# Products of the values for all chunks issued beside the first products of the levels, old state added by VectorE, last level on blocks of 32

## The reference

```python
def rwkv_scan(r, w, k, v, a, b, s0):
    def step(S, inp):
        r_t, w_t, k_t, v_t, a_t, b_t = inp
        sa = jnp.einsum('bhij,bhj->bhi', S, a_t)
        S = S * w_t[:, :, None, :] + sa[..., None] * b_t[:, :, None, :] + v_t[..., None] * k_t[:, :, None, :]
        return S, jnp.einsum('bhij,bhj->bhi', S, r_t)
...
def trunk_layer(x, l, v_first, past, p):
    h = x @ p['w_in'][l]
...
    merged = jax.nn.sigmoid(g_a) * (o_a @ p['w_up_a'][l]) + jax.nn.sigmoid(g_b) * (o_b @ p['w_up_b'][l])
    y = layer_norm(ALPHA * x + merged @ p['w_out'][l], p['ln_g'][l], p['ln_b'][l])
```

## Time and profile before

| | |
|---|---|
| Time, median of 3 runs | 2416.53 us (2414.43 to 2420.03) |
| Time of the profiled execution | 2419.8 us |
| Its span, first to last instruction | 2418.1 us |
| Busy: TensorE, VectorE, ScalarE | 2350.2, 610.7, 364.4 us |
| Mean granted clock of TensorE | 0.989 |

### The profile page before, as it was taken

How to read it: one execution, slowest core, us unless ns; L and a number is a source line. 1 busy time by engine, 2 the same in 40 slices (tenths; PEclk the granted TensorE clock), 3 DMA queues, 4 the chain that set the end, 5 groups by cost and what they waited for, 6 DMA issues and landing times.

```text
span 2418.1 us, 39663 instructions
## 1 busy us (share of the span) xinstructions
PE 2350.2 (97%) x17860; PEld 1906.4 (79%) x17860; DVE 610.7 (25%) x1076; ACT 364.4 (15%) x939; POOL 131.5 (5%) x233
## 2 busy tenths in 40 slices
PE   8999999999999999999899999999999999999995
PEld 7887878778787788888788778787787867888884
DVE  0132322217216410111201323222163153101112
ACT  0021111111113310000201211111201143100002
POOL 0000000002011110000000000000010112100000
PEclk9999999999999999999899999999999999999997
DMA  6532332327343354444244323323373334544441
GB/s 212 193 123 84 112 116 97 124 89 281 125 140 96 119 187 154 143 142 154 91 153 141 103 91 105 122 91 107 116 257 123 130 105 144 170 153 143 143 153 71
DMA packets 86793, 326.41 MB, mean 135 GB/s; under 512 B 11808, under 2 KB 11824, under 8 KB 84448
## 3 DMA queue, kind: packets, MB, share of 16 engines
q1 hardware_dynamic: 73152, 266.44, 33.8%
q0 software_dynamic: 13472, 57.43, 6.6%
HBM read 313.39 MB, written 18.82 MB: 137 GB/s over the span
## 4 chain that ended last, share of the span: by engine, by line
PE 94%; DVE 2%; ACT 2%; DMA 1%; issue 0%; POOL 0%; DVEq 0%; ACTq 0%; SPq 0%; POOLq 0%
PE PB L520 74%; PE PB L747 3%; PE PB L622 2%; PE PB L591 1%; PE PB L490 1%; PE PB L631 1%; DMA WT<-in_w_all 1%; PE PB L905 1%; PE PB L794 1%; PE PB L607 1%; PE PB L839 1%; PE PB L633 1%; ACT ARENA L914 1%; PE PB L652 1%; PE PB L659 1%; PE PB L644 0%
## 5 line engine op out<-in xcount | busy, mean ns | idle before, releaser
L520 PE MATMUL PB<-XT,WT 128*128 128x264 f32 (+1 forms) x6016 | 1426.9, 392 | 16.2 <-DMA WT<-in_w_all 7.8
L520 PEld LDWEIGHTS PB<-XT,WT 128*128 128x128 f32 (+1 forms) x6016 | 1118.4, 190 | 239.8 <-issue 37.5
L520 PE MATMUL PB<-H,WT 128*128 128x264 f32 x2048 | 456.5, 386 | 3.1 <-DVE H L1571 3.1
L520 PEld LDWEIGHTS PB<-H,WT 128*128 128x128 f32 x2048 | 389.0, 190 | 70.3 <-issue 3.8
L914 ACT ACTIVATE ARENA<-PB 128x512 f32<-128x512 f32 (+6 forms) x197 | 95.3, 500 | 410.0 <-PE PB L622 175.1
L1568 DVE SCALAR_TENSOR_TENSOR H<-H,PB 128x264 f32<-128x264 f32 x32 | 13.7, 429 | 305.2 <-PE PB L520 305.2
L392 POOL DMA_DIRECT2D out<-in_c_win x16 | 8.2, 510 | 1338.1 <-DVE ARENA L1327 1338.1
L1181 DVE COPY SHO<-PB 128x9 f32<-128x9 f32 x66 | 11.0, 167 | 266.5 <-ACT H L936 215.0
L1147 ACT ACTIVATE ARENA<-XT 128x1056 f32<-128x1056 f32 x8 | 8.7, 1083 | 458.5 <-DVE XT L1592 458.0
L936 ACT ACTIVATE H<-PB,PD 128x264 f32<-128x264 f32 x58 | 27.8, 479 | 275.2 <-PE PB L520 275.1
L951 ACT ACTIVATE H<-PB 128x264 f32<-128x264 f32 x64 | 24.9, 389 | 293.9 <-PE PB L520 293.7
(11 more groups left out here) (275 smaller groups left out, 1736.6 us busy)
## 6 DMA issues: line engine op xcount, KB each, us to landing
WT<-in_w_all SPq DMA_DIRECT2D x504, 512.0 KB, 4.7
out<-in_c_win POOLq DMA_DIRECT2D x16, 512.0 KB, 5.1
ARENA<-in_c_cmp POOLq DMA_DIRECT2D x64, 128.0 KB, 4.3
ARENA<-in_c_sel POOLq DMA_DIRECT2D x64, 128.0 KB, 3.4
ARENA<-in_c_win POOLq DMA_DIRECT2D x32, 256.0 KB, 3.6
ARENA<-in_states POOLq DMA_DIRECT2D x4, 1024.0 KB, 8.2
out<-ARENA POOLq DMA_DIRECT2D x4, 1024.0 KB, 5.4
ARENA<-in_w1d POOLq DMA_DIRECT2D x4, 1024.0 KB, 5.2
```

The source lines that it names most:

```text
L520: ins = mm(PB[0:m, bank, 0:T], WT[:, s, k, 0:m], x, start=start, stop=stop)
```

## The change

It does four things, all in the delta rule of the prompt.

The products of the values (lines 646, 661 and 671 before), which don't depend on the state, leave the chunks. A new function `of_values` issues them for all four chunks inside the `y` steps of levels 1, 2 and 3, one behind each product of the level, into banks 1, 2 and 3, where each chunk now has its own columns (`cq`). The chunks' own products add to what lies there (`start=False`).

The identity times the old state (line 663) is gone. VectorE multiplies the old state by the decay ahead of time (`d`, into `STD`), and after `s` computes decay times PSUM plus `STD` with two instructions of 128x64 (`stt`) in the place of one of 128x128.

The announcement of `s` comes behind 4 products in the place of 12. A chunk has 20 products in the place of 36.

The last level works on blocks of 32: its `y` and `z` steps have as many products as before, 16 each, but of 32x32. ScalarE copies half as much for it, and VectorE adds two pieces of 32 partitions.

```diff
-        assert used[0] <= at_chunks + 6400
+        LT = take(P, 2 * NCH, C)
+        RS, US, STD = take(P, 2, C), take(P, 2, C), take(P, 2, C)
...
               a="th exp sv tok0 tok1 x2 " + " ".join(f"y{j}" for j in lv) + " " + " ".join(f"r{c} u{c} o{c}" for c in ch),
               v=lambda it: ("lw one gate cum " + ("vd vg vm " if it >= NQUAD else "") + "kb kf kp rk at rt bt kt bon g40 g41 x0 x1 lm1 "
-                            + " ".join(f"lm{j + 1} z{j}" for j in range(1, LEVELS)) + f" z{LEVELS} st " + " ".join(f"s{c}" for c in ch)))
+                            + " ".join(f"lm{j + 1} z{j}" for j in range(1, LEVELS)) + f" z{LEVELS} st " + " ".join(f"d{c} s{c}" for c in ch)))
...
+                    def of_values(j, q, ra):
...
+                        w, c = divmod(q, NCH)
+                        k = (2 * w + 1) * NCH + c
+                        weights = {1: G4[ra, k, 0, :], 2: TOK[ra, 0, w, c, :], 3: TOK[ra, 2, w, c, :]}[j]
+                        x = G4[ra, k, 1, :] if j == 2 else TOK[ra, 0, w, c, :]
+                        return mm(PB[ra, j, q * C:q * C + C], weights, x, start=q == 0, stop=True, skip_group_check=True)
...
                     for j in lv:
                         wait(("rw_v", f"lm{j}" if j == 1 else f"z{j - 1}"))
...
+                        if j == 2:
+                            wait(("rw_a", "tok1"))
                         for q, ra in eight:
-                            ins = mm(PB[ra, 0, q * C:q * C + C], LM[other(ra), q, :], XX[other(ra), q, :], start=True, stop=True)
+                            oa = other(ra)
+                            if j < LEVELS:
+                                ins = mm(PB[ra, 0, q * C:q * C + C], LM[oa, q, :], XX[oa, q, :], start=True, stop=True)
+                            else:
+                                ins = mm(PB[low(ra), 0, q * C:q * C + 32], LM[up(oa), q, 32:C], XX[up(oa), q, 0:32], start=True, stop=True)
+                            if j <= 3:
+                                of_values(j, q, ra)
                         mark("rw_t", it, ins, f"y{j}")
                         project(L, hq, f"y{j}")
                         wait(("rw_a", f"y{j}"),)
...
                             for ra in both:
-                                ins = mm(PB[ra, 5, cols], YY[ra, q, :], XX[ra, 2 * NCH + q, :], start=True, stop=True)
+                                if j < LEVELS:
+                                    ins = mm(PB[ra, 5, cols], YY[ra, q, :], XX[ra, 2 * NCH + q, :], start=True, stop=True)
+                                else:
+                                    ins = mm(PB[up(ra), 5, q * C + 32:q * C + C], YY[low(ra), q, 0:32], XX[low(ra), 2 * NCH + q, 32:C],
+                                             start=True, stop=True)
                         mark("rw_t", it, ins, f"z{j}")
...
 
                     wait(("rw_a", "tok1"), ("rw_v", "st"))
                     for c in ch:
-                        pairs = [(w, slice(w * C, w * C + C)) for w in range(2)]
+                        pairs = [(w, slice((w * NCH + c) * C, (w * NCH + c + 1) * C)) for w in range(2)]
                         if c:
                             wait(("rw_v", f"s{c - 1}"))
-                        for w, cw in pairs:
+                        for w, cq in pairs:
                             for ra in both:
-                                mm(PB[ra, 0, cw], AR[ra, w * NCH + c, 0, :], ST[ra, c % 2, w, :], start=True, stop=False)
-                            for ra in both:
-                                ins = mm(PB[ra, 0, cw], G4[ra, (2 * w + 1) * NCH + c, 0, :], TOK[ra, 0, w, c, :], start=False, stop=True)
+                                ins = mm(PB[ra, 1, cq], AR[ra, w * NCH + c, 0, :], ST[ra, c % 2, w, :], start=False, stop=True, skip_group_check=True)
                         mark("rw_t", it, ins, f"r{c}")
                         project(L, hq, f"r{c}")
                         wait(("rw_a", f"r{c}"))
-                        for w, cw in pairs:
+                        for w in range(2):
                             for ra in both:
-                                ins = mm(PB[ra, 1, cw], XX[ra, (2 + w) * NCH + c, :], RS[ra, w, :], start=True, stop=True)
+                                ins = mm(PB[ra, 0, w * C:w * C + C], XX[ra, (2 + w) * NCH + c, :], RS[ra, w, :], start=True, stop=True)
                         mark("rw_t", it, ins, f"u{c}")
                         project(L, hq, f"u{c}")
                         wait(("rw_a", f"u{c}"))
-                        for w, cw in pairs:
+                        for w, cq in pairs:
                             for ra in both:
-                                mm(PB[ra, 3, cw], TOK[ra, 1, w, c, :], US[ra, w, :], start=True, stop=False)
+                                ins = mm(PB[ra, 3, cq], TOK[ra, 1, w, c, :], US[ra, w, :], start=False, stop=True, skip_group_check=True)
+                        mark("rw_t", it, ins, f"s{c}")
+                        for w, cq in pairs:
                             for ra in both:
-                                mm(PB[ra, 3, cw], TOK[ra, 2, w, c, :], TOK[ra, 0, w, c, :], start=False, stop=False)
+                                mm(PB[ra, 2, cq], ST[ra, c % 2, w, :], AR[ra, w * NCH + c, 1, :], start=False, stop=True, skip_group_check=True)
+                        for w, cq in pairs:
                             for ra in both:
-                                ins = mm(PB[ra, 3, cw], small(EYE)[ra], ST[ra, c % 2, w, :], start=False, stop=True)
-                        mark("rw_t", it, ins, f"s{c}")
-                        for w, cw in pairs:
-                            for ra in both:
-                                mm(PB[ra, 2, cw], ST[ra, c % 2, w, :], AR[ra, w * NCH + c, 1, :], start=True, stop=False)
-                            for ra in both:
-                                mm(PB[ra, 2, cw], US[ra, w, :], G4[ra, 2 * w * NCH + c, 1, :], start=False, stop=False)
-                            for ra in both:
-                                ins = mm(PB[ra, 2, cw], TOK[ra, 0, w, c, :], G4[ra, (2 * w + 1) * NCH + c, 1, :], start=False, stop=True)
+                                ins = mm(PB[ra, 2, cq], US[ra, w, :], G4[ra, 2 * w * NCH + c, 1, :], start=False, stop=True, skip_group_check=True)
                         mark("rw_t", it, ins, f"o{c}")
...
-                        mark("rw_a", it, copy(YY.rearrange("p q n -> p (q n)"), PB[:, 0, :]), f"y{j}")
+                        n = C if j < LEVELS else 32
+                        mark("rw_a", it, copy(YY[:, :, 0:n], PB[:, 0, :].rearrange("p (q n) -> p q n", n=C)[:, :, 0:n]), f"y{j}")
                         take_out(L, hq, f"y{j}")
                         take_out(L, hq, f"z{j}")
                     for c in ch:
                         wait(("rw_t", f"r{c}"))
-                        mark("rw_a", it, copy(RS.rearrange("p w n -> p (w n)"), PB[:, 0, 0:P]), f"r{c}")
+                        mark("rw_a", it, copy(RS[:, :, :], of_chunk(1, c)), f"r{c}")
...
-                        mark("rw_a", it, copy(US.rearrange("p w n -> p (w n)"), PB[:, 1, 0:P]), f"u{c}")
...
+                        mark("rw_a", it, copy(US.rearrange("p w n -> p (w n)"), PB[:, 0, 0:P]), f"u{c}")
...
-                        mark("rw_a", it, copy(H[:, hp:hp + 2, c * C:c * C + C], PB[:, 2, 0:P].rearrange("p (w n) -> p w n", n=C)), f"o{c}")
+                        mark("rw_a", it, copy(H[:, hp:hp + 2, c * C:c * C + C], of_chunk(2, c)), f"o{c}")
...
                         else:
-                            v(f"z{j}", tt(xt, xt, z[:, 2 * NCH:4 * NCH, :], ALU.add))
+                            for a in range(2):
+                                up = slice(a * C, a * C + 32)
+                                x = xt[up, :, 32:C]
+                                ins = tt(x, x, z[up, 2 * NCH:4 * NCH, 32:C], ALU.add)
+                            v(f"z{j}", ins)
...
-                        wait(("rw_t", f"s{c}"))
-                        v(f"s{c}", tt(ST[:, (c + 1) % 2], PB[:, 3, 0:P].rearrange("p (w n) -> p w n", n=C),
-                                      spread(decay[:, :, c], P, 2, C), ALU.mult))
+                        wait(f"s{c - 1}" if c else "st")
+                        v(f"d{c}", tt(STD[:, :, :], ST[:, c % 2], spread(decay[:, :, c], P, 2, C), ALU.mult))
+                        wait(("rw_t", f"s{c}"), f"d{c}")
+                        for w in range(2):
+                            ins = stt(ST[:, (c + 1) % 2, w, :], PB[:, 3, (w * NCH + c) * C:(w * NCH + c + 1) * C], GP[:, w * NCH + c, C:C + 1], STD[:, w, :],
+                                      ALU.mult, ALU.add)
+                        v(f"s{c}", ins)
                         mix(L, hq, f"s{c}")
```

More of the change, by code:

```diff
@@ L253, in hybrid_trunk @@
         KF = RK
-        used[0] = at_chunks + 6400
+        used[0] = at_chunks + 6528
         SV = take(P, 6, C)
@@ L260, in hybrid_trunk @@
         TOK = take(P, 6, NCH * C).rearrange("p (i w) (c n) -> p i w c n", w=2, n=C)
```

(7 more changed lines are left out.)

## The result

The changed kernel takes 2382.27 us (median of 4 runs, 2376.52 to 2383.60) and the kernel before 2417.97 us beside it. The ratio is 0.985 with a 95% interval of 0.9833 to 0.9867, so 36 us or 1.5% less. The forecast was 2380.4 us.

What follows compares the result with a forecast made beforehand. TensorE's own queue was taken as the bound, busy 2350.2 of 2418.1 us. Terms -30.0 + 0.2 - 6.9 + 0.6 = -36.1 us from the median 2416.53 gave 2380.4 us, range 2375.5 to 2391, at 80%.

Steps and rivals of the forecast that it cites:

- The chunks: Delta rule chunks: each of 32 loses 16 two-quarter products of 0.0585 us, 0.936 us a chunk, 30.0 us in all.
- The values: Steps y1 to y3: 16 added products alternate with the level's on four quarters, 1.09 for 1.08 us, 0.2 us in all.
- The rival in which they take turns with the level: Blocks y1 to y3: paired products go one at a time, 2.02 us a block, +22.5 us, so 2403; chance 5%.
- The last level: Steps y5 and z5: blocks of 32x32 products take 0.65 us in place of 1.08; 16 blocks save 6.9 us.
- The rule of the Trainium skill: Last level, kept as rival: some 60 cycles' overhead per matmul, so 32 columns save almost nothing; 2387 us, chance 10%.
- the forecast's four cycles a column and product: Price of moving columns, read from records of 264 columns: 32 x 4 cycles at 2.4 GHz make 53 ns.
- the short rows: Profile rows with 8 and 15 moving columns, 32 output columns: 17 and 14 ns a product with four strips at work.
- The waits: TensorE's waits: none new in covered chunks; in each layer's fourth quad a new 0.3 us for VectorE, 0.6 us in all.
- the forecast's terms: Whole change: chunks -30.0, values +0.2, last level -6.9, new waits in uncovered chunks +0.6 us, sum -36.1 us.

Runs made afterwards that it cites:

- control run: The changed kernel itself, run again without edits on the same chip as the two runs before it: 2378.59 us, ratio 0.9839 to the kernel before.

## Why the prediction was right

**The chunks.** 16 products of 0.0585 us were to go from each of 32 chunks, 0.936 us. The period fell by 0.93. The experiment that takes 12 of them away and the one that brings 4 back give 2.77 and 0.93 us a quad, which is the same price to 1%.

**The values.** Held: 1.09 us a block. The rival in which they take turns with the level (22.5 us more) isn't seen; their own second place, behind the level, shows the price of leaving two quarters idle.

**The last level.** The forecast was 0.65 us a block, from products with 8 and 15 moving columns; it was 0.62, at the end of 29 ns a product, and 0.90 us a quad in place of 0.86. The part alone gave 7.05 us over both layers, of 6.9 predicted. The rule of the Trainium skill (TensorEngine Tiling (Array Packing), Instruction Overhead), by which one column is as slow as 60, doesn't hold for these fp32 products if it is counted in columns: by it the block would have stayed near 1.0. Counted in cycles, of which the same section gives some 60 as each product's overhead, it isn't refuted. By the forecast's four cycles a column and product, a record has two, so 32 columns are 64 cycles of a record, and in one strip or tile a record took 34, 29 and 29.5 ns with 8, 15 and 32 columns. The pace of the short rows was already that of 32 columns. The reason that I gave was only half of it. I took the moving columns for the pace; the experiment with 64 columns of weights and 32 moving ones (1.05 us) shows that the weights' columns set it just as well. Both of my rows had 32 columns of weights and few moving ones, and so gave the right number, in part by luck. Whether it is the 32 columns of weights or a fixed cost of a record that holds 8, 15 and 32 moving columns at the same pace, no run separates.

**The waits.** No new one in a covered chunk. The one that was there, at the first `r` of each layer's first quad, was left alone by the forecast and grew from 1.53 to 1.64 us, which is why these quads got 0.1 us less:

```profile
PE PB L667 <- DVE ARENA L1342: 3.3, 2, 1.6
```

In the uncovered chunk VectorE's pair took 0.48 us (0.5 predicted), and it is late:

```profile
521.25 0.31 PEld L667 LDWEIGHTS PB<-ARENA 64*64 64x64 f32 x8 [0.34 <-DVE ARENA L1348]
...
522.90 0.45 PE L679 MATMUL PB<-ARENA 64*64 64x64 f32 x8 [0.38 <-ACT ARENA L929]
...
523.18 0.40 PE L683 MATMUL PB<-ARENA 64*64 64x64 f32 x8
...
523.39 0.48 DVE L1351 SCALAR_TENSOR_TENSOR ARENA<-PB,ARENA 128x64 f32<-128x64 f32 x2 [2.34 <-PE PB L679]
...
523.93 0.45 PE L667 MATMUL PB<-ARENA 64*64 64x64 f32 x8
```

The `s` row starts 0.28 us ahead of line 683, VectorE runs 523.39 to 523.87, and the next `r` starts at 523.93. Without the wait it would stand 0.25 us earlier, where `o` ends. The forecast was 0.3. The chunk takes 523.93 - 521.25 = 2.68 us, 0.65 less than the 3.33 between 538.06 and 541.39 before; the forecast's terms give 0.94 - 0.3 = 0.64.

**What the sum left out.** The fourth quad of the first layer got only 3.88 us shorter and that of the second 4.27, though the program is the same. In the first layer the clock takes part. The granted clock behind chunk 2 of the first layer, before and then after:

```profile
543.00:545.00 2.00, 1.61 (x48) 1.48 (x48) 0.29 (x1) 0.29 (x2) 0.23 (x1) 1.00 0.02 6
545.00:548.00 3.00, 2.78 (x17) 2.51 (x18) 1.52 (x5) 2.32 (x7) 3.00 (x6) 1.00 0.59 188
```

```profile
524.00:525.80 1.80, 1.05 (x22) 0.77 (x24) 0.20 (x1) 0.69 (x3) 0.00 (x0) 1.00 1.01 414
525.80:528.90 3.10, 2.73 (x32) 2.35 (x29) 0.87 (x4) 0.69 (x3) 2.04 (x4) 0.51 0.49 152
```

Before, TensorE was busy 1.61 of 2.00 us in the last window of the uncovered chunks and kept 1.00. Afterwards it was busy 1.05 of 1.80 us, since the same waits for ScalarE stand between shorter blocks, and the clock was at 0.51 behind it, close to the lower of its two levels (1.2 of 2.4 GHz). In the control run the windows behind have 0.78 and 0.65. It costs 0.4 us up to the transposes; in the control it came later and the fourth quad took 87.92 us, 4.28 less than before. What it costs behind the transposes wasn't measured.

The idle time alone doesn't decide it. The run with the values' transposes beside `x2` and no other change has the same last chunks. At the same place TensorE was busy for the same 1.05 of 1.80 us, and the clock behind stayed at 1.00:

```profile
520.45:522.25 1.80, 1.05 (x23) 0.77 (x25) 0.20 (x1) 0.69 (x3) 0.00 (x0) 1.00 0.89 362
522.25:525.35 3.10, 2.72 (x38) 2.43 (x35) 1.91 (x7) 1.72 (x5) 2.06 (x4) 1.00 0.52 151
```

Over all runs, the six executions with these uncovered chunks of 20 products have twelve ends of a layer, and the clock fell at five of them. It fell at none of the eight ends with chunks of 24 or 36 products (the kernel before, the last level alone, the values alone, the identity back) and at none of the six with covered chunks. That makes the shorter uncovered chunks likely to have a part in it, but no run isolates them. The sum over the quads, 35.6 us against the 36.1 of the forecast, has these 0.4 us in it. The forecast's terms make 4.57 us a quad and 0.6 us back for the new waits; the quads in the middle gave 4.60, which makes 0.2 us more over all eight, the first quads' wait took 0.2 back and the low clock 0.4. The total is as close as it is because these are small and partly cancel.

The difference between the two spans, 38.5 us, agrees less well with the forecast than the sum of the quads does, and it is the worse measure: 2.9 us of it are in code that the change doesn't touch, where the clock was low for a shorter time.

## What to carry to other kernels

Where an engine's own queue is the bound, price its instructions from the order in time of blocks with different counts: two blocks gave 0.0585 us a product and 0.146 us a block, and that held within 2% in the changed kernel and the four variants that took such products away or added some. Where one group stood behind the other it was too high, 0.93 for 0.75 us. Products that use only part of the array were free where they stood in turn with products for the other part, not one group behind the other; look for operands that don't depend on the running state and can be moved there. When a chain gets faster, look at where its cover was thin, and when filler is moved, at where the boundaries of what it fills then fall.

## What the runs showed of the hardware that I had not expected

TensorE started products of one quarter ahead of products of another that stand in front of them in the program, for some 0.17 us at the border of two groups of 16.

An fp32 product in a tile of at most 64x64 takes the longer of what its moving columns and its weights' columns ask for: with two tiles at work 16 products took 0.62 us with 32 of both, 1.01 with 64 moving, 1.05 with 64 of weights, and 1.08 with 64 of both.

The granted clock fell to its lower level behind the last chunk of the first layer in both executions of the changed kernel, and not in the second layer, where the same program kept 1.00. With the same last chunks it fell at five of twelve places, once behind a stretch in which TensorE was busy 1.05 of 1.80 us, and not behind another of the same 1.05 of 1.80 us. In the unchanged 800 us between the delta rules the time follows it: 799.5 us with 23.9 us at the lower level, 794.2 with 6.8.
